# One-core two-block kernel: the conditioning sums of the merge stage move from TensorE to VectorE

## The reference, cut to what matters

```
mod_x = (silu(c) @ ada_w[l] + ada_b[l])[:, None, :]          # ada_w: 1024 x 6144
sh1, sc1, gt1, sh2, sc2, gt2 = split(mod_x, 6)
...                                                          # second block, for l = 0, 1:
mod = silu(c_2) @ ada_w_2[l] + ada_b_2[l]                    # ada_w_2[l]: 1024 x 3072
```

```
u, v = split(gelu(z_sgu), 2);  v = layer_norm(v, sgu_ln_g, sgu_ln_b)      # per chunk of 128 tokens
v = einsum('gpq,bnqgc->bnpgc', sgu_w, v) + sgu_b.T[:, :, None]            # "mix": 8 groups g
y_s = u * v
g_a, g_s = split(sigmoid(z_gate), 2)
merged = g_a * (y_a @ w_branch_a) + g_s * (y_s @ w_branch_b)
x = layer_norm(ALPHA * x + gt1 * (merged @ w_out), ln1_g, ln1_b)
```

## Time and profile before

| what | value |
|---|---|
| median of three timed runs | 3654.74 us |
| lowest and highest | 3651.61 and 3655.66 us |
| span of the profiled execution | 3649.4 us |
| mean granted TensorE clock | 0.945 |
| merge, from the first weights of v to the last matmul of y | 1238.1 to 1724.3 us |
| PE busy over the whole span | 3241.2 us, 89% |
| DVE busy over the whole span | 1053.5 us, 29% |

### The profile page before, as it was taken

How to read it: one execution, slowest core, us unless ns; L and a number is a source line. 1 busy time by engine, 2 the same in 40 slices (tenths; PEclk the granted TensorE clock), 3 DMA queues, 4 the chain that set the end, 5 groups by cost and what they waited for, 6 DMA issues and landing times. The chain is left out here.

```text
span 3649.4 us, 69770 instructions
## 1 busy us (share of the span) xinstructions
PE 3241.2 (89%) x31414; PEld 1926.8 (53%) x31414; DVE 1053.5 (29%) x2259; ACT 620.2 (17%) x1274; POOL 249.0 (7%) x249
## 2 busy tenths in 40 slices
PE   6799999999999899998788898889884986899987
PEld 3587787787788544443533333323332443455553
DVE  2333333333333101013402101111104334234442
ACT  1122122122121111000100000000001334023331
POOL 1111111111111000000000000000000112010000
PEclk8899999999999999899799999999997998899998
DMA  4100000000000355332599999999992120243311
GB/s 149 39 16 11 20 16 12 19 17 16 15 4 4 133 186 184 115 138 81 218 428 428 426 425 426 430 430 422 424 410 70 38 68 2 71 77 67 66 34 75
DMA packets 202427, 566.36 MB, mean 155 GB/s; under 512 B 42669, under 2 KB 130243, under 8 KB 177576
## 3 DMA queue, kind: packets, MB, share of 16 engines
q1 hardware_dynamic: 202120, 562.12, 40.2%
q10 hardware_dynamic: 32, 0.03, 0.0%
HBM read 559.56 MB, written 2.27 MB: 154 GB/s over the span
## 5 line engine op out<-in xcount | busy, mean ns | idle before, releaser
L1990 PE MATMUL bank<-ex_ring,xe 128*64 128x512 f32 x2048 | 476.9, 620 | 97.5 <-DMA ex_ring<-in_exp_w_dram 92.0
L1990 PEld LDWEIGHTS bank<-ex_ring,xe 128*64 128x64 f32 x2048 | 170.1, 142 | 401.8 <-issue 388.8
L1990 PE MATMUL bank<-ex_ring,hidT 128*64 128x512 f32 x1024 | 226.9, 598 | 5.3 <-DMA ex_ring<-in_exp_w_dram 5.1
L643 PE MATMUL bank<-hT,wj 128*128 128x512 f32 x384 | 195.5, 636 | 5.8 <-DVE vj L1363 2.9
L2162 DVE TENSOR_TENSOR ex_acc<-ex_acc,bank 128x512 f32<-128x512 f32 x64 | 44.0, 687 | 511.4 <-PE bank L2026 511.4
L2849 PE MATMUL bank<-h2T_mixer,na_w 128*128 128x512 f32 x384 | 177.4, 610 | 13.1 <-DMA na_w<-in_odd_w_in_dram 13.1
L2461 PE MATMUL bank<-h2T_mixer,ev_w 128*128 128x512 f32 x320 | 155.9, 640 | 29.0 <-DMA ev_w<-in_even_w_in_dram 20.9
L1636 PE MATMUL bank<-hT,mg_ring 128*128 128x512 f32 x384 | 167.7, 594 | 0.0
L1311 DVE TENSOR_TENSOR pm<-bank,m_level 128x512 f32<-128x512 f32 x120 | 82.9, 691 | 225.1 <-PE bank L747 224.7
L1990 PEld LDWEIGHTS bank<-ex_ring,hidT 128*64 128x64 f32 x1024 | 72.8, 138 | 141.4 <-issue 138.5
L763 PE MATMUL bank<-XT,pm 64*64 64x32 f32 x3840 | 134.8, 221 | 0.8 <-DVE pm L1311 0.8
(11 more groups left out here) (468 smaller groups left out, 4888.1 us busy)
## 6 DMA issues: line engine op xcount, KB each, us to landing
ex_ring<-in_exp_w_dram SPq DMA_DIRECT2D x192, 2048.0 KB, 17.7
cond_w<-in_ada_w_dram SPq DMA_DIRECT2D x20, 2048.0 KB, 10.9
mg_ring<-in_w_in_dram SPq DMA_DIRECT2D x8, 2048.0 KB, 7.6
na_w<-in_odd_w_in_dram SPq DMA_DIRECT2D x32, 512.0 KB, 6.1
wj<-in_w_in_dram SPq DMA_DIRECT2D x24, 512.0 KB, 3.8
ev_w<-in_even_w_in_dram SPq DMA_DIRECT2D x24, 512.0 KB, 7.0
ada_ring<-in_ada_w_dram SPq DMA_DIRECT2D x4, 2048.0 KB, 19.7
na_bias<-na_table_dram SPq DMA_DIRECT2D x32, 224.0 KB, 6.3
```

What stands on the lines that cost most here:

```text
L643: last = mm(PROJ[:], wj[:, c, i, :], hT[:, c, 0:T], start=(c == 0), stop=(c == KT - 1))
L1990: r[e] = mm(out[a, :], lhs[j][:, a], w[:, j, 512 * c:512 * c + 512], start=(first and j == 0), stop=(last and j == len(lhs) - 1), skip_gro ...
```

## The change

A new class WeighedSums takes the place of Conditioning in the merge. Conditioning stays for the four chunks of the first stage.

- The weights still lie with eight rows of the matrix on each partition. DVE now does the sum over those eight rows: one multiplication by the partition's factor silu_c[:, j] and seven multiply-and-adds (L239, L241, L243), each 128x512, each waiting for the one before. That gives 128x512 sums, in one of four buffers.
- PE adds the 128 partitions: sixteen matmuls a chunk with a 128x32 piece of the sums as weights and a single column of ones moving (L255). They stand in groups of three chunks (48 matmuls) after outputs 5, 9, 13, 17, 21 and 25, and two chunks after output 29.
- Each chunk is loaded in two halves of 1 MB, each freed by DVE when it has read it. SP queues three chunks behind each of the main chunks 1 to 6 and two behind main chunk 7; before, the last chunks were loaded up to main chunk 13.
- The mix bias is no longer a matmul. DVE adds it from gate_bias, a 128x1024 tile that a DMA fills with sgu_b on every partition, and then multiplies by u: two operations in place of one.
- The copies by ACT and the writes to banks 4 and 5 are gone.

```
+class WeighedSums:
+    W, SUMS = 512, 4
+    def load(self, sp, i):
+        w, c, _ = self.chunks[i]
+        rows = w.rearrange("(p h j) n -> p h j n", h=2, j=KT // 2)
+        for h in range(2):
+            if i:
+                sp.wait_ge(self.half_read[h], i)
+            sp.dma_start(self.w[:, h], rows[:, h, :, c:c + self.W]).then_inc(self.half_in[h], 16)
+    def weigh(self, dve, i):
+        own = self.own = self.own or Steps(dve, self.steps)
+        _, _, which = self.chunks[i]
+        acc = self.sums[:, i % self.SUMS, :]
+        if i >= self.SUMS:
+            dve.wait_ge(self.turned, i - self.SUMS + 1)
+        for j in range(KT):
+            h = j // (KT // 2)
+            if j % (KT // 2) == 0:
+                dve.wait_ge(self.half_in[h], 16 * (i + 1))
+            w, factor = self.w[:, h, j % (KT // 2), :], self.k.sT[:, j, which:which + 1]
+            if j == 0:
+                own.last(dve.tensor_scalar(acc, w, factor, None, ALU.mult))
+            elif j < KT - 1:
+                own.last(dve.scalar_tensor_tensor(acc, w, factor, acc, ALU.mult, ALU.add))
+            else:
+                dve.scalar_tensor_tensor(acc, w, factor, acc, ALU.mult, ALU.add).then_inc(self.summed, 1)
+            if j == KT // 2 - 1:
+                dve.sem_inc(self.half_read[0], 1)
+        dve.wait_ge(self.summed, i + 1)
+        dve.sem_inc(self.half_read[1], 1)
+    def to_channels(self, pe, i):
+        pe.wait_ge(self.summed, i + 1)
+        per = self.W // P
+        for f in range(per):
+            for g in range(4):
+                c = slice(32 * g, 32 * g + 32)
+                last = pe.matmul(self.out[c, i * per + f:i * per + f + 1], self.sums[:, i % self.SUMS, f * P + 32 * g:f * P + 32 * g + 32],
+                                 self.k.ones[:, 0:1], start=True, stop=True, skip_group_check=True)
+        last.then_inc(self.turned, 1)
...
+    conds_after = {c: range(3 * c - 3, min(3 * c, len(ADA))) for c in range(1, 8)}
+    conds_turned = {4 * c + 1: conds_after[c] for c in conds_after}
...
-                    sp.dma_start(sb_row[:], A["sgu_b"]).then_inc(S["sgu_in"], 16)
+                    sp.dma_start(gate_bias[:], A["sgu_b"][0].partition_broadcast(P)).then_inc(S["sgu_in"], 16)
...
-                while conds < len(ADA) and c and sorted(cond_at)[conds] <= weighted[4 * c - 1]:
-                    cond.load(sp, conds)
-                    conds += 1
+                for n in conds_after.get(c, ()):
+                    cond.load(sp, n)
...
-                    mm(o.rearrange("p (n t) -> p n t", n=NX), k.ones[0:1, :], sb_row[0:1, n:n + 1, :].to_broadcast([1, NX, P]),
-                       start=True, stop=False)
                     for t in range(NX):
-                        last = mm(o[:, t * P:t * P + P], v[:, t, n * P:n * P + P], swT[:, n, :], start=False, stop=(t == NX - 1))
+                        last = mm(o[:, t * P:t * P + P], v[:, t, n * P:n * P + P], swT[:, n, :], start=True, stop=True)
...
-                if i in cond_at:
-                    if cond_at[i] == SECOND[0] + 1:
-                        pe.wait_ge(cond.added, 1)
-                    cond.product(pe, cond_at[i])
-                if i - 2 in cond_at and cond_at[i - 2] == SECOND[-1]:
-                    cond.to_channels(pe, SECOND[-1])
+                for n in conds_turned.get(i, ()):
+                    cond.to_channels(pe, n)
...
-                if i - 1 in cond_at:
-                    cond.move_row(act, cond_at[i - 1])
...
+            for n in (*conds_after[1], *conds_after[2]):
+                cond.weigh(dve, n)
             for i in range(2):
                 dve.wait_ge(S["w_turned"], i + 1)
...
             stats(v, range(NX))
+            for n in (*conds_after[3], *conds_after[4]):
+                cond.weigh(dve, n)
             norm(v, range(NX), 1, S["v_normed"])
+            for n in (*conds_after[5], *conds_after[6], *conds_after[7]):
+                cond.weigh(dve, n)
             cond.add_bias(dve, FIRST, 2 * KT, 2 * KT)
+            cond.add_bias(dve, SECOND, 6 * KT, 8 * KT)
...
-                if (kind, n) == ("y", 6):
-                    cond.add_bias(dve, SECOND, 6 * KT, 8 * KT)
...
-                    dve.tensor_tensor(ys[:, n, :], u[:, n, :], o, ALU.mult).then_inc(S["moved_dve"], 1)
+                    own.last(dve.tensor_tensor(by_chunk(ys[:, n, :]), by_chunk(o), gate_bias[:, n:n + 1, :].to_broadcast([P, NX, P]), ALU.add))
+                    dve.tensor_tensor(ys[:, n, :], ys[:, n, :], u[:, n, :], ALU.mult).then_inc(S["moved_dve"], 1)
```

More of the change, by code:

```diff
@@ L199, in add_bias, with __init__ @@
                           self.k.cols1[:, bias:bias + n].unsqueeze(2).to_broadcast([P, n, 3]), ALU.add).then_inc(self.added, 1)
+class WeighedSums:
+    W, SUMS = 512, 4
+    def __init__(self, k, s, chunks, bank):
+        self.k, self.chunks = k, chunks
+        per = self.W // P
+        self.out = bank[:, 0:per * len(chunks)]
+        self.w = k.sb("ws_w", [P, 2, KT // 2, self.W], s)
+        self.sums = k.sb("ws_sums", [P, self.SUMS, self.W], s)
+        self.half_in = [k.sem(f"ws_half_in{h}") for h in range(2)]
+        self.half_read = [k.sem(f"ws_half_read{h}") for h in range(2)]
+        self.summed, self.turned, self.added, self.steps = (k.sem("ws_" + x) for x in "summed turned added steps".split())
+        self.own = None
+    def load(self, sp, i):
[28 more added lines that the diff above has]
+        pe.wait_ge(self.summed, i + 1)
+        per = self.W // P
+        for f in range(per):
[4 more added lines that the diff above has]
+        last.then_inc(self.turned, 1)
+    def add_bias(self, dve, chunks, at, bias):
+        per, which = self.W // P, self.chunks[chunks[0]][2]
+        n, lo = len(chunks) * per, chunks[0] * per
+        dve.wait_ge(self.turned, len(self.chunks))
+        dve.tensor_tensor(self.k.mod[:, at:at + n, which], self.out[:, lo:lo + n], self.k.cols1[:, bias:bias + n],
+                          ALU.add).then_inc(self.added, 1)
@@ L1556, in stage_merge @@
     NB = 4
-    ADA = [(A["ada_w"][0], c) for c in range(2 * D, 6 * D, 512)]
+    ADA = [(A["ada_w"][0], c, 0) for c in range(2 * D, 6 * D, 512)]
     FIRST = range(len(ADA))
-    ADA += [(A["ada_w_2"][l], c) for l in range(2) for c in range(0, 3 * D, 512)]
+    ADA += [(A["ada_w_2"][l], c, 2) for l in range(2) for c in range(0, 3 * D, 512)]
     SECOND = range(len(FIRST), len(ADA))
-    weighted = [i for i, o in enumerate(outs) if o[2] is not None]
-    twice = len(ADA) - (len(chunks) - 1)
-    cond_at = sorted(weighted[1:-4:4] + weighted[3:4 * twice:4])
-    cond_at = {i: n for n, i in enumerate(cond_at)}
+    conds_after = {c: range(3 * c - 3, min(3 * c, len(ADA))) for c in range(1, 8)}
+    conds_turned = {4 * c + 1: conds_after[c] for c in conds_after}
     names = """x_in sgu_in ln1_in w_turned w_moved made moved_act moved_dve v_normed stats std used row_mm row_moved
@@ L1576, in stage_merge @@
         swT = k.sb("swT", [P, 8, P], s)
-        sb_row = k.sb("sb_row", [1, 8, P], s)
+        gate_bias = k.sb("gate_bias", [P, 8, P], s)
         gain = k.sb("gain", [P, 2, D], s)
@@ L1584, in stage_merge @@
         rs = k.sb("mg_rs", [P, NX], s)
-        cond_w = k.sb("cond_w", [P, KT * 512], s)
-        cond = Conditioning(k, s, "c2", ADA, [cond_w[:]], (4, 5), 6)
+        cond = WeighedSums(k, s, ADA, bank[6])
         v = x1
@@ L1592, in _ @@
         def _(sp):
-            conds = 0
             for c, src in enumerate(chunks):
@@ L1749, in _ @@
                     dve.wait_ge(S["moved_act"], 16)
-                    dve.tensor_tensor(ys[:, n, :], u[:, n, :], o, ALU.mult).then_inc(S["moved_dve"], 1)
+                    by_chunk = lambda view: view.rearrange("p (n t) -> p n t", n=NX)
+                    own.last(dve.tensor_tensor(by_chunk(ys[:, n, :]), by_chunk(o), gate_bias[:, n:n + 1, :].to_broadcast([P, NX, P]), ALU.add))
+                    dve.tensor_tensor(ys[:, n, :], ys[:, n, :], u[:, n, :], ALU.mult).then_inc(S["moved_dve"], 1)
                 elif kind == "a":
```

## The result

The changed kernel took 3590.89 us (median of 4 runs, 3588.28 to 3591.96), the kernel before beside it 3653.18 us (4 runs, 3648.87 to 3655.66). The ratio is 0.9832 with an interval of 0.9819 to 0.9846: faster by 1.7%, 62 us. The forecast was 3605 us with a range that began at 3595: the direction was right and the gain was larger than the range allowed. One execution of a later kernel (the mix alone) took 11330.86 us at a granted clock of 1.0 where its six others took 3631 to 3636 us; its cause is not known, and no ratio here counts it.

What follows compares the result with a forecast made beforehand. PE's own stream was taken to bound the merge; -55.2 + 19.2 - 16.7 - 1.6 + 1.0 + 3.4 = -49.9 us off the median of 3654.7 gave 3604.8 us, range 3595 to 3633 us.

Steps and rivals of the forecast that it cites:

- products and turning removed: Merge on PE: twenty chunks' products and turnings between outputs go, 2.76 us each, 55.2 us off.
- 640 one-column records: Sixteen matmuls a chunk adding up partitions on PE: 0.03 us a record, 19.2 us added, at least 18 us.
- mix: Mix stage without bias matmuls, paced by two DVE operations an output: 8.3 us instead of 25.0, 16.7 us off.
- first outputs of a: First two a outputs, right after the mix: 1.6 us off if the clock no longer falls in the mix.
- wait at the transposes: PE's wait for DVE's copy of the transposed gate weights, behind chunk 5: from 0.78 to about 1.7 us, 1 us lost.
- clock behind the groups: Seven groups of one-column matmuls may lower PE's clock: two falls of 1.7 us taken, 3.4 us added.
- The cover of the other groups: At each other group PE comes 41 us after the main chunk's issue, sums ready after 33: hidden by 8 us.
- The slower one: Rival, chance 0.06: weight loads of neighbouring column groups don't overlap, 0.139 us a record, 89 us, kernel at 3675 us.
- The late DVE: Rival, chance 0.12: halves land 3 us later each, PE waits some 10 us at the transposes, kernel at 3614 us.

Runs made afterwards that it cites:

- the mix alone: Kernel before with only the mix bias moved from PE matmuls to DVE, the conditioning staying on PE: 3632.82 us, ratio 0.9957 to before.
- the wide version: Changed kernel with four matmuls of 128x128 weights per chunk in place of sixteen of 128x32: 3598.36 us, ratio 0.9856 to before.
- the two banks: Changed kernel with the second four transposes sent to bank 5, so PE need not wait for DVE's copy: 3579.3 us, ratio 0.9813 to before.
- the whole chunks: Changed kernel, but both halves of a conditioning chunk load only when DVE has read the whole chunk: 3618.74 us in its one run.

## Why the prediction was wrong

By its own steps, as terms of the merge on PE:

| term | predicted, us | measured, us |
|---|---|---|
| products and turning removed (both from rows of before) | -55.2 | -55.2 |
| 640 one-column records | +19.2 | +6.3 |
| mix | -16.7 | -17.0 |
| first outputs of a | -1.6 | -1.6 |
| wait at the transposes | +1.0 | +5.6 |
| clock behind the groups | +3.4 | 0 |
| clock behind the wait | none | +1.2 |
| merge starts earlier | none | -0.7 |
| sum | -49.9 | -61.4, of 62.8 |

Most of the last 1.4 us lies in small steps between outputs: those of a and b, without the products and turnings between them, take 116.1 us before and 113.5 us after, 1.1 us more than the first two outputs explain. Why is open.

**The step that failed is the pace of the added records, 0.03 us, and with it the sentence "Nothing makes it less than 18 us, since that is the densest row of small matmuls that I have".** The value was taken from the scan's 64x64 tiles with "four tiles of the array in use, as here". But each head of the scan has its operands and its output on the same half, so its two heads take turns on two tiles only. With two diagonal tiles the experiment gives 0.030 us, with four of 64x64 0.016, and with four column groups of 128x32 0.0098 us. So of the 12.9 us between 19.2 and 6.3, some 9 are the number of tiles and some 4 the narrower weights, which the prediction named and gave no price. A second error sits on top: the densest row that a kernel happens to contain is a bound on nothing, since no row showed the form in question. The span was missed by 12.9 us too, but only because the other errors cancel, and that is luck.

**The clock.** Rows 13 and 14 made a fall look possible, and two at 1.7 us were booked. None came, nor behind any of the seven groups of up to 2.6 us in the wide version. This does not refute the term as it was reckoned, for groups of 2.9 us: the groups took 0.94 us, and a burst of 2.89 us on two tiles was followed by a clock of 0.52 and an output of 15.63 us. What else lowered the clock in this stage were the bias matmuls, idle waits of PE of a few us, gaps on issue, and the long burst of 128x128 records.

**The wait at the transposes.** The mechanism was named, and its size was off: 6.36 us, not 1.7. DVE's copy came 1.7 us later than reckoned (done at 1303.76, against 1301.4 + 0.7). PE reached the place at 1297.46 instead of 1300.5, since it started 0.7 us earlier and its groups were 2 us shorter. So what the first group saved was given back as waiting. As the two banks show, the clock took 1.2 us more.

**The cover of the other groups** was given as 8 us each. It was 1.4 us at the fifth group and 2 us at the sixth. The prediction put the normalisation of v behind chunk 11 and asked only whether the mix would wait for it. It left out that these 12 us of DVE's queue stand ahead of chunk 12 and so move the next chunks and their loads late. Nothing was lost by it here, but with four more operations a chunk PE waited 10.75 us there.

**The rivals.** The slower one needed 0.113 us a record, and the measured 0.0098 rules it out: weight loads of 109 ns do overlap across column groups that share all their rows. This goes against the Trainium skill, TensorE: Matmul & The Clock Gate, section "The mechanism", by which a load overlaps a matmul in flight only where the row groups differ.

In these groups a matmul of the program (two records) took 20 ns. From the Trainium skill, TensorE: Matmul & The Clock Gate, section "Wait — 56ns, not 53.3ns?", some 62 ns of sequencer time a matmul without hardware decode, I had estimated 40 us. That took each of the 640 records for a matmul; with the program's 320 matmuls the estimate from that page is 19.8 us. The trace agrees with neither. The long bursts come near 62 ns: 144 matmuls in 8.0 us (56 ns), 288 in 18.2 us (63 ns). But that average is made of a fast first part and gaps. A group of 48 ends before the first gap.

The late DVE was right in place and wrong in price: as long as the halves load beside the reading, the loss stays at 6.8 us. And its cause was another: the loads came 1.1 to 1.5 us later than reckoned and not 3 us each, and the larger part of the wait is that PE was 3.0 us earlier at the place.

## What to carry to other kernels

Before taking a price for a small matmul from another part of a trace, write down which tiles of the array both use in turn and how wide their weights are; among the forms measured here, the first moves the price from 0.030 to 0.016 us and the second from there to 0.010. Where no row shows the form, the range must be open on the cheap side too. When work moves to an idle engine, its average idle share says little: list what is queued ahead of each place where the busy engine waits, and give such a place its own buffer first, which here took 8.9 us off the merge up to y for a few changed lines.

## What the runs showed of the hardware

- Records of 170 ns and weight loads of 109 ns each started every 9.8 ns. So the cost of such small records is read from the distance of their starts and not from their duration.
- With one column moving, a record's price times the number of tiles in turn was 0.033 to 0.040 us for weights of 32 columns, 0.060 to 0.063 for 64, and 0.107 for 128.
- With 128x32 weights in four column groups, 1 and 32 moving columns cost the same (0.0099 us a record), and 128 cost 0.029.
- Behind a dense output PE took 174, 237 and 140 small records of three bursts at once, then paused 4.70, 5.09 and 1.34 us on issue. In the longer two it paused again after every 128 records.
- The bias matmuls with one weight row cost more than their own time: eight of them take 8.4 us at full clock, and the mix was 17 to 19 us longer with them, since the granted clock fell to 0.5 in it.
- Nine idle stretches of PE in this stage, of 3.12 to 19.05 us (6.36 us in the changed kernel), were each followed by outputs of 15.0 to 16.4 us instead of 13.9. The waits of 1.70 and 0.79 us ahead of y were followed by 55.10 us of y in six kernels, by 56.21 us in the changed one and by 55.80 us with the whole chunks. Why these differ is open.
- The clock also fell with PE never idle: behind 2.89 us of 64x64 records on two diagonal tiles, and within a burst of 128x128 records with one column moving. It did not behind 2.90 us of 128x64 records.
